# Two stacked transformer blocks on one core: the second layer's norm re-ordered, the last feature weights loaded from ScalarE's queue, the output product's rows ordered by mixer, and weight units dealt by step

## What is computed

```python
hl = xl * (1.0 + scale_l) + shift_l
yl, yc = even_mixer(...)            # layer 0: pooling and a recurrent scan
yl, _ = odd_mixer(...)              # layer 1: attention with a gate
xl = layer_norm(DEEPNORM_ALPHA * xl + gate_l * yl, ln_g[l], ln_b[l])
```

```python
q, k, v, g, lr, u_f, u_h, u_s = jnp.split(rms_norm_2(x, norm_g[l, 0]) @ w_in[l], split_at, axis=-1)
mix = jnp.concatenate([y_a, y_b, y_c, y_d], axis=-1)   # gated linear attention, Fourier, hyena, short convolution
x = x + mix @ w_out[l]
x = x + cross_attention(rms_norm_2(x, norm_g[l, 1]), mem_n, w_xq[l], w_xkv[l], w_xo[l])
x = x + swiglu(rms_norm_2(x, norm_g[l, 2]), w_gate_up[l], w_down[l])
return rms_norm_2(x, final_norm_g)
```

## Time and profile before

| what | value |
|---|---|
| time, median of 3 runs (lowest, highest) | 3949.34 us (3944.61 to 3950.49) |
| the profiled execution's own time | 3950.59 us |
| its span | 3948.7 us |
| TensorE busy with products | 3620.2 us (92%) |
| VectorE, ScalarE, GpSimd busy | 2022.7 (51%), 1541.9 (39%), 272.2 us (7%) |
| TensorE's mean granted clock (1 is full speed) | 0.962 |
| DMA traffic | 548.76 MB, 139 GB/s over the span |

### The profile page before, as it was taken

The page is one execution under the profiler, slowest core; times in us unless marked ns, Lnnn a source line. Parts: engine busy times, 40 slices in busy tenths (PEclk is TensorE's granted clock), DMA queues, the critical chain, the costliest instruction groups (busy, mean ns, idle before and its releaser), DMA issues. The chain is left out here.

```text
span 3948.7 us, 73924 instructions
## 1 busy us (share of the span) xinstructions
PE 3620.2 (92%) x32796; PEld 2974.7 (75%) x32796; DVE 2022.7 (51%) x3453; ACT 1541.9 (39%) x2586; POOL 272.2 (7%) x311
## 2 busy tenths in 40 slices
PE   6789999999898998989989799888999999999998
PEld 3566676767676676767678688846989799999887
DVE  1444454444445447675565546656544455555444
ACT  1333343333333333354454444334543444444343
POOL 0001110111011113012000000100000000000000
PEclk8899999999999999989999899989999999999999
DMA  9523333242333406443224444323554445555554
GB/s 322 179 78 94 105 90 115 69 125 72 117 105 92 129 19 251 141 139 103 89 97 161 144 150 144 124 92 126 178 183 144 159 163 184 185 179 187 187 186 155
DMA packets 349484, 548.76 MB, mean 139 GB/s; under 512 B 11724, under 2 KB 119916, under 8 KB 346988
## 3 DMA queue, kind: packets, MB, share of 16 engines
q1 hardware_dynamic: 346860, 539.83, 42.4%
q10 hardware_dynamic: 2304, 4.20, 0.3%
HBM read 535.86 MB, written 8.13 MB: 138 GB/s over the span
## 5 line engine op out<-in xcount | busy, mean ns | idle before, releaser
L301 PE MATMUL lane<-r,r 128*128 128x256 f32 (+1 forms) x8520 | 1500.4, 325 | 31.8 <-DVE r L259 25.4
L301 PE MATMUL bank<-r,r 128*128 128x512 f32 (+2 forms) x6360 | 1407.0, 360 | 43.1 <-DVE r L259 34.5
L259 DVE TENSOR_TENSOR r<-ring,r 128x1024 fp32r<-128x1024 f32 x773 | 947.9, 1233 | 944.0 <-ACT r L298 942.7
L301 PEld LDWEIGHTS lane<-r,r 128*128 128x128 f32 x8520 | 1259.2, 190 | 205.2 <-DVE r L259 34.4
L301 PEld LDWEIGHTS bank<-r,r 128*128 128x128 f32 x6360 | 1049.5, 194 | 259.9 <-issue 55.5
L298 ACT ACTIVATE r<-ring 128x1024 fp32r<-128x1024 f32 x773 | 810.5, 1055 | 955.4 <-PE lane L301 555.5
L301 PE MATMUL lane<-arena 64*64 64x64 f32 (+5 forms) x13708 | 667.9, 249 | 60.1 <-issue 24.0
L301 PEld LDWEIGHTS lane<-arena 64*64 64x64 f32 (+3 forms) x13708 | 505.0, 139 | 209.2 <-issue 126.3
L298 ACT ACTIVATE arena<-lane 128x256 f32<-128x256 f32 (+3 forms) x578 | 252.7, 457 | 582.9 <-PE lane L301 484.0
L270 DVE COPY arena<-lane 128x256 f32<-128x256 f32 (+3 forms) x366 | 131.7, 362 | 307.5 <-PE lane L301 304.4
L259 DVE TENSOR_TENSOR arena<-arena 128x256 f32<-128x256 f32 (+6 forms) x546 | 253.6, 495 | 27.7 <-ACT arena L298 14.8
(11 more groups left out here) (93 smaller groups left out, 1328.6 us busy)
## 6 DMA issues: line engine op xcount, KB each, us to landing
ring<-in_mod_w SPq DMA_DIRECT2D x96, 1024.0 KB, 5.4
ring<-in_w_gate_up SPq DMA_DIRECT2D x88, 1024.0 KB, 5.1
ring<-in_ev_w_in SPq DMA_DIRECT2D x44, 1024.0 KB, 8.6
ring<-in_w_down SPq DMA_DIRECT2D x44, 1024.0 KB, 5.2
ring<-in_od_w_in SPq DMA_DIRECT2D x40, 1024.0 KB, 5.1
ring<-in_w_in SPq DMA_DIRECT2D x40, 1024.0 KB, 5.1
ring<-in_w_xkv SPq DMA_DIRECT2D x32, 1024.0 KB, 5.2
ring<-in_ev_w_out SPq DMA_DIRECT2D x28, 1024.0 KB, 5.0
```

The source lines that it names most:

```text
L259: return Nothing() if self.e is None else self.e.tensor_tensor(o, a, b, op)
L301: return Nothing() if self.e is None else self.e.matmul(o, l, r, start=start, stop=stop)
```

## The change

Parts, in the order of the list:

1. `Group.rot` becomes a list of starts (`order`). For the first block's product it is the same order as before; for `w_out_2` it is blocks 0, 4, 12, 8 in place of 12, 0, 4, 8.
2. The norm: the first tile is aggregated and scaled behind its last residual, its root is finished within the second tile's last residual. The gains run tile by tile. ScalarE squares quarters of 512 columns, each behind its gain. The two sums and both roots of the RMS norm are taken together. The fence `block2` becomes a mark, on which SP and GpSimd wait in `load_mix`.
3. The convolutions of `uh_in` become steps of their own (`uh_conv`): chores for the first two groups, four steps behind the product for the third. `local_mixers` yields its share of units with each step. The splits of the mixed rows wait for the hyena's input product (mark `first_norm_read`) and, from block 12 on, for `sc_out`; four of them stand ahead of the last convolutions. The filter's steps move one unit later, and two units instead of three stand behind `hy_norm`.
4. Two units of the key product instead of one stand ahead of the norm.
5. `load_fg` moves behind the down product's first column group and is issued by ScalarE. `x_gain` multiplies by the gain, ahead of the root, for the first three column groups, as chores.
6. At the end, `last_sum` takes the sums and roots of both tiles, then VectorE scales 1536 columns of the first tile, ScalarE 1536 of the second, VectorE the last 512 of both; SP stores 1536 and 512 columns.

```diff
-    def __init__(self, act_, kt, tiles, w, c0, n, kind, args, done, is_feats, rot):
+    def __init__(self, act_, kt, tiles, w, c0, n, kind, args, done, is_feats, order):
...
+        self.order = order or list(range(0, kt, 4))
+    def row(self, k):
+        return self.order[k // 4] + k % 4
...
-    step("fence", "block2")
+    step("mark", "block2")
...
-    drain(normed("hF0", "xk", 0, turn_all, ("norm1",)))
+    drain(normed("hF0", "xk", 0, turn_all, ("norm1",), summed=True))
...
+    def uh_done(n):
+        def f():
+            if n < 2:
+                for i in range(4):
+                    chores.append(later(step, "uh_conv", i, n))
+        return f
...
             for g2 in range(2):
                 step("fn_channels", tl, g2, bank(aux))
-                yield
+                yield 1
         for tl in range(2):
             step("fn_tokens", tl, bank(aux))
-            yield
+            yield 1.2
...
         for f in range(4):
             step("sc_conv", f)
-            yield
+            yield 0.9
+        yield 2.4
         b = bank(aux)
         step("sc_sum", b)
-        yield
+        yield 0.5
         step("sc_root", b)
-        yield
+        yield 2.6
         step("sc_out", b)
 
-    weave(local_mixers(), to_hyena, 1.5)
+    weave(local_mixers(), to_hyena)
...
-                        (lambda: step("x3_done")) if n == 3 else None, 12) for n in range(4)], Turn([0, 1, 2, 3]), (2, 12))
+                        (lambda: step("x3_done")) if n == 3 else None, [0, 4, 12, 8]) for n in range(4)], Turn([0, 1, 2, 3]), (2, 12))
...
     drain(to_hyena)
+    step("mark", "first_norm_read")
+    splits(4)
+    for f in range(4):
+        step("uh_conv", f, 2)
     step("local_done")
     step("mark", "hyena")
...
     def hyena():
-        splits(4)
+        splits(2)
         yield 1
         splits(2)
         yield 1
-        step("hy_one", bank(hy_turn))
-        splits(2)
-        yield 1
-        step("hy_two", bank(hy_turn))
         splits(2)
         yield 1
         splits(2)
+        step("hy_one", bank(hy_turn))
+        yield 1
+        step("hy_two", bank(hy_turn))
+        yield 1
...
         for tl in range(2):
             step("hy_norm", tl)
-        yield 3
+        yield 2
...
     next(kv)
+    next(kv)
     weave(normed("hF16", "xk", 16, aux, ("x3",)), kv, 1)
...
-    groups[-1].done = lambda: step("load_fg")
...
+            if n == 0:
+                step("load_fg")
+            if n < 3:
+                chores.append(later(step, "x_gain", n))
...
+    finish_chores()
+    for tl in range(2):
+        step("last_sum", tl)
     for tl in range(2):
         step("finish", tl)
```

In VectorE's program:

```diff
+        st = M.st2[:, 32 * tl:32 * tl + 32]
+        residual(M.xk[:, tl, n * 512:n * 512 + 512], b, M.gb1, st, n,
+                 (lambda: norm_root("norm1", 0, M.st2[:, 0:32])) if (tl, n) == (1, 3) else None)
+        if n == 3:
+            norm_root_in("norm1", tl, st)
...
-        norm_roots("norm1", [M.st2[:, 32 * tl:32 * tl + 32] for tl in range(2)])
-        for q in range(4):
-            for tl in range(2):
-                norm_gain("norm1", q, tl, M.xk[:, tl, :], M.lng1, M.lnb1)
+        for i, (tl, q) in enumerate((tl, q) for tl in range(2) for q in range(4)):
+            if i == 1:
+                norm_root("norm1", 1, M.st2[:, 32:64])
+            norm_gain("norm1", q, tl, M.xk[:, tl, :], M.lng1, M.lnb1)
...
+    def x_gain(n):
+        c_ = slice(512 * n, 512 * n + 512)
+        v.wait_ge(*at("fg"))
+        for tl in range(2):
+            v.wait_ge(*at("sq", "x5", n, tl))
+            v.tt(M.xk[:, tl, c_], M.xk[:, tl, c_], M.fg[:, c_], MUL).then_inc(*v.n(("x_gain", n, tl)))
```

In ScalarE's program:

```diff
-            split(name, k, ("fence", "hyena", "pe"), ("sc_out",))
+            split(name, k, ("fence", "first_norm_read", "pe"), *([("sc_out",)] if k >= 12 else []))
...
+        for q in range(4):
+            x(0, q)
+        x(1, 0)
+        for q in range(1, 4):
+            x(1, q)
+            norm1_square(0, q - 1)
+        norm1_square(0, 3)
+        for q in range(4):
+            norm1_square(1, q)
...
+    def load_fg():
+        a.wait_ge(*at("gate_up_read"))
+        a.dma(M.fg, row(M.I["final_norm_g_2"])).then_inc(*a.n(("fg",), sem="ld_fg", by=16))
...
+    def finish(tl):
+        if tl == 1:
+            a.wait_ge(*at("x_gain", 2, 1))
+            a.wait_ge(*at("fin_pow", tl))
+            a.act(M.xk[:, tl, 0:1536], M.xk[:, tl, 0:1536], ACT.Copy, scale=M.st2[:, 41 + 2 * tl:42 + 2 * tl]) \
+                .then_inc(*a.n(("result", tl, 0)))
```

More of the change, by code:

```diff
@@ L1026, in out_groups @@
     def out_groups(tiles, ns):
-        return [rows("mix", KT, tiles, "ev_w_out", n * 512, 512, "add_first", (n,), None, 8) for n in ns]
+        return [rows("mix", KT, tiles, "ev_w_out", n * 512, 512, "add_first", (n,), None, [8, 12, 0, 4]) for n in ns]
     out_lat = stream(out_groups([2, 3], [1]) + out_groups([2, 3, 0, 1], [0]) + out_groups([2, 3], [2, 3]), out_turn, (2, 8))
@@ L1239, in gla @@
             step("to_mix", "gla", 0, j, bank(aux))
-    to_hyena = stream([feats("hF0", KT, "w_in_2", W2_H + 512 * n, "uh_in", (n,)) for n in range(3)], st_turn)
+    def uh_done(n):
[4 more added lines that the diff above has]
+        return f
+    to_hyena = stream([feats("hF0", KT, "w_in_2", W2_H + 512 * n, "uh_in", (n,), uh_done(n)) for n in range(3)], st_turn)
     def beside_gla():
@@ L1267, in local_mixers, with splits @@
             step("sc_conv", f)
-            yield
+            yield 0.9
+        yield 2.4
         b = bank(aux)
         step("sc_sum", b)
-        yield
+        yield 0.5
         step("sc_root", b)
-        yield
+        yield 2.6
         step("sc_out", b)
-    weave(local_mixers(), to_hyena, 1.5)
+    weave(local_mixers(), to_hyena)
     fill = stream([rows("mF", KT, [0, 1], "w_out_2", n * 512, 512, "add_x", ("x3", n, None),
-                        (lambda: step("x3_done")) if n == 3 else None, 12) for n in range(4)], Turn([0, 1, 2, 3]), (2, 12))
+                        (lambda: step("x3_done")) if n == 3 else None, [0, 4, 12, 8]) for n in range(4)], Turn([0, 1, 2, 3]), (2, 12))
     hy_turn = Turn([4, 5, 6, 7])
+    early = [0, 1, 2, 3, 4, 5, 6, 7, 12, 13, 14, 15]
+    def splits(n):
+        for _ in range(n):
+            step("split", "mF", early.pop(0))
     drain(to_hyena)
+    step("mark", "first_norm_read")
+    splits(4)
+    for f in range(4):
+        step("uh_conv", f, 2)
     step("local_done")
@@ L1284, in order_of_work @@
     step("hy_load")
-    early = [12, 13, 14, 15, 0, 1, 2, 3, 4, 5, 6, 7]
-    def splits(n):
-        for _ in range(n):
-            step("split", "mF", early.pop(0))
     def hyena():
-        splits(4)
+        splits(2)
         yield 1
@@ L1382, in order_of_work, with down_done, f @@
                    feats("hF32", KT, "w_gate_up_2", DFF + 512 * n, "ff_up", (n,))]
-    groups[-1].done = lambda: step("load_fg")
-    groups += [rows("ff", FT, [0, 1], "w_down_2", n * 512, 512, "add_x", ("x5", n, 1)) for n in range(4)]
+    def down_done(n):
+        def f():
+            if n == 0:
+                step("load_fg")
+            if n < 3:
+                chores.append(later(step, "x_gain", n))
+        return f
+    groups += [rows("ff", FT, [0, 1], "w_down_2", n * 512, 512, "add_x", ("x5", n, 1), down_done(n)) for n in range(4)]
     feed_forward = stream(groups, Turn(list(range(8))))
@@ L1502, in load_mem @@
         load("mem", M.memx, I["mem_2"][0].rearrange("(t p) n -> p t n", p=P))
-    def load_fg():
-        sp.wait_ge(*sp.table.at("gate_up_read"))
-        load("fg", M.fg, row(I["final_norm_g_2"]))
     def finish(tl):
@@ L2412, in gate_diag, with residual @@
                 .then_inc(*v.n(("gate_diag", l, side_, q)))
-    def residual(xs, b, gate, stats, n):
+    def residual(xs, b, gate, stats, n, between=None):
         v.tt(M.bank[b[0]], M.bank[b[0]], gate[:, n * 512:n * 512 + 512], MUL).then_inc(*v.n())
@@ L2417, in residual @@
         v.stt(xs, xs, ALPHA, M.bank[b[0]], MUL, ADD).then_inc(*v.n(("free", *b)))
+        if between:
+            between()
         own()
@@ L2579, in rms @@
         if summed:
-            v.wait_ge(*at("at_rms", dst, tl, "act"))
-            v.wait_ge(*at("at_rms", dst, tl))
+            if after[0] == "norm1":
+                sums = range(2) if tl == 0 else ()
+                for i in sums:
+                    for q in range(4):
+                        v.wait_ge(*at("norm1_sq", i, q))
+            else:
+                sums = (tl,)
+                v.wait_ge(*at("at_rms", dst, tl, "act"))
+                v.wait_ge(*at("at_rms", dst, tl))
             own()
-            v.add_up(c, M.st2[:, 44 + 4 * tl:48 + 4 * tl]).then_inc(*v.n())
+            for i in sums:
+                v.add_up(M.st2[:, 4 * i:4 * i + 1], M.st2[:, 44 + 4 * i:48 + 4 * i]).then_inc(*v.n())
             own()
@@ L2586, in rms @@
             v.wait_ge(*at("rms_sq", dst, tl))
-        root(r, c, 1.0 / D, RMS_EPS, "rms_in", dst, tl)
```

(7 more changed lines are left out.)

74 lines of the change are left out of this document (44 added, 30 removed).

## The result

The changed kernel takes **3922.46 us** in the median of 4 runs (3918.92 to 3929.13), against 3949.2 for the kernel before in runs beside it: a ratio of 0.9931, with an interval of 0.9914 to 0.9947. That is faster by 0.69%. Forecast were 3929.1 us and a range of 3919.5 to 3940.5. Its profiled execution took 3925.52 us, with a span of 3923.7, 25.0 less than the span before.

What follows compares the result with a forecast made beforehand. TensorE, busy 92% of the span, was taken as the bound, so only its gaps could be won. Terms -5.0 - 9.4 - 4.0 + 0 - 6.5 + 5.8 - 1.1 = -20.2 us gave 3929.1 us from the median 3949.34; range 3919.5 to 3940.5.

Steps and rivals of the forecast that it cites:

- Part 1, -5.0 us: Second layer's norm: earlier first-tile root and quarter squares let transposes start at 2246.5, not 2251.49; bounds -3.5 and -6 us.
- Part 2, the taps, -9.4 us: Mixers' end and hyena's filter: VectorE's queue lets the taps' products start at 2580.9, not 2590.35; ends -4 and -12 us.
- Part 2, two units instead of three, -4.0 us: Behind the hyena's norm: transposes follow at once instead of waiting for a third unit; bounds 0 and -4.1 us.
- Part 3, 0: Cross attention's norm: a second key unit ahead only moves the 3.33 us gap; ends 0 and -3.3 us.
- Part 4, -6.5 us: Change-over to the down product: load leaves SP's queue, so the 4.83 us gap and 1.7 us of clock go.
- rival to part 4: Change-over to the down product stays late: only issue time, 0.34 us, is gained; 3935.3 us; chance 0.06.
- Part 5, +5.8 us: Down product's first column group: x_gain waits for the weights, 4.1 us idle plus 1.7 of clock; ends 0 and +8.1.
- Part 6, -1.1 us: Kernel's end: operands ready by 3942, but stores bound it, the last landing at 3947.1; ends 0 and -4 us.
- The likeliest case: Whole kernel: all terms sum to -20.2 us, giving 3929.1 us; own range 3924 to 3935, chance 0.53.
- none of the rivals: Features in time 0.17; hyena's start unmoved 0.17; late change-over 0.06; VectorE bounds mixers 0.04; little change 0.03.
- signs of being wrong: Forecast wrong if new gap missing or over 8 us, taps under 10 us earlier, or clock below 1 within mixers.
- the rival for which that sign stood: Mixers: VectorE becomes the bound and TensorE's clock falls, up to 49 us more; 3958 us; chance 0.04.

Runs made afterwards that it cites:

- Runs 5: The norm's change alone, on the kernel before: norm gap 19.90 us, not 25.17; from TensorE's restart to the turned low-rank rows 21.38 us, not 24.52.
- run 6: The mixers' change alone, on the kernel before: turned low-rank rows to taps 303.68 us (before 314.34), taps to transposes behind the hyena's norm 97.31 (before 102.39).
- Run 8: run 1 with 136 identity transposes on TensorE ahead of the norm's first transposes: restart to turned low-rank rows 21.24 us, 0.1 less.
- run 7: Kernel before with two sets of 40 identity transposes on TensorE in the gaps at the mixers' end: mixers' sum to taps 33.15 us, not 37.47.
- run 1: Changed kernel with its first two gains one output group later: first down product to last product 247.52 us, not 254.73; whole 3921.66 us.
- run 3: run 1 with the final norm's weights loaded from SyncE's queue behind the last up product, as before: first down product to last product 253.38 us.
- run 4: Changed kernel with the old finish, without x_gain, load still on ScalarE's queue: last product to span's end 11.81 us against 10.00; whole 3925.42 us.
- run 10: run 1 with one unit of keys ahead of the cross attention's norm, not two: gap 3.53 us.
- run 11: Changed kernel with the final norm's weights loaded five units into the down product's first column group and one more key unit behind the second tile's norm step: 3924.57 us.
- run 9: run 2 with TensorE's mark for the load set behind the last up product: first down product to last product 247.53 us.
- run 12: Changed kernel unaltered, measured again beside run 11: 3928.59 us, 0.9946 of before.
- run 2: run 1 with the final norm's weights loaded from SyncE's queue, still behind the down product's first column group: first down product to last product 254.10 us.

## Why the prediction held, step by step

**Part 1, -5.0 us: -5.3, and 3.1 more that it had no term for.** The steps of the norm held one by one. The clock behind the stop was left out, although the prediction priced the same effect at 1.7 us at three other places. Runs 5 and 6 put the 3.1 us in this part. The windows show them as clock: the upper level begins 1.5 us sooner behind the restart and lasts 2 us longer from there, some 3.4 us more of it in all. Run 8 shows that a busier TensorE in the stop doesn't add to it. Why the level is held longer behind the shorter stop stays open.

**Part 2, the taps, -9.4 us: -10.8.** The input product's end was forecast 2.0 us earlier (+1.2 - 1.5 - 1.7) and came 1.5 earlier: its last product was over at 2559.30 before and at 2550.22 after, 283.3 and 281.8 us behind the turned low-rank rows. From there to the first sine 15.3 us were forecast and 13.9 measured, to the taps 23.6 and 21.8. The step said that TensorE's units fit beneath and don't set the end. In the kernel before they did set it in part: run 7 gets 3.3 of these us by keeping the clock up alone. The size was nearly right, the account of where the old time had gone was not whole.

**Part 2, two units instead of three, -4.0 us: -4.0** behind the cut in run 6. The step that failed is "from the taps to the hyena's norm the chain stays as it is": with four splits of the rows fewer between the filter's steps the gap of 1.85 us is gone, which is worth 1.1 us. In the changed kernel's first profile another 1.2 came on top, from the clock alone. It falls at the taps in every profile, and how long it stays down changes between runs of the same code: ahead of the cut the kernels with part 2 had 0.91 in 37.2 to 37.6 us, 0.83 in 39.7 (runs 1, 3 and 4) and 0.79 in 39.76 (run 6), and their C was 94.5 to 97.3 us. These 1.2 us are chance as far as is known.

**Part 3, 0: 0.** The gap is 3.32 us with two units ahead of the norm and 3.53 with one (run 10): a unit ahead of the norm only moves it. One behind the second tile's norm step breaks it up, into 0.83 and 1.79 (run 11), and that is bounded by the weights' splits.

**Part 4, -6.5 us: -5.9** by run 3 against run 1. 0.81 us of the 4.83 stayed, and the forecast had taken off all of it. Issued by SyncE behind a wait that is already met, the same load costs 0.01 us more than from ScalarE (run 9). That agrees with the Trainium skill, DMA: Bandwidth & Descriptors, section Issuing engines are not separate DMA queues. As a rival to part 4 its rule would have missed by 5.6 us, since what the change removed was a wait.

**Part 5, +5.8 us: +7.2** by run 1, +6.2 in run 12. The chain is the forecast's: load behind the column group, wait, late split of the third unit, TensorE dry, clock. Two of its terms were mis-sized. The load left 1.2 us behind the group's last product (3722.85 against 3721.63), not 2.0: ScalarE issued it while its second square was still running. And it took 7.1 us to land, not 5.3, near the 7.7 that stood as the upper end. The gap is 5.05 for 4.1, the clock 2.2 for 1.7.

**Part 6, -1.1 us: -1.8** by run 4, bounded by the stores as forecast, at 400 GB/s.

The likeliest case came and none of the rivals. The sum, -20.2, is 4.8 short of the -25.0 between the two spans: 3.1 in stretch A, 2.3 in C, 1.4 in B, 0.7 at the end and 0.4 in the rest came on top, 2.2 in the down product and 0.9 ahead of the norm went the other way. So part of the closeness is luck: terms that were left out (3.1 of clock, 1.1 of splits) and terms that were mis-sized partly cancel. The median of 3922.46 us lies below the likeliest case's own range of 3924 to 3935, within the wide one; the second median of the same kernel, 3928.59 (run 12), lies in both. Of the signs of being wrong, the new gap is 5.05 us, between its two bounds, and the taps start 18.4 us earlier, over the 10. The third, a clock below 1 within the mixers, came in the letter: 0.66 in the 5 us from 2466 on, at the end of the linear attention. But the kernel before has the same 0.66 there, from 2482 on, and through the short mixers, from 2471 to 2572, it is 1.00 in the changed kernel's first profile: the rival for which that sign stood did not come. (It can fall there for a moment: to 0.72 over 6 us from 2525 and again from 2556 in run 2, whose stretch B is the long one, and to 0.66 over 5 us from 2558 in run 12.) The claim that 0.2% can be told from no change was too good for one part: medians of 5 or 6 runs did not show 7 us that the trace shows.

## What to carry to other kernels

A wait in the queue that feeds the weights costs by its place, not by the transfer behind it; before a step is moved, look up what its mark on the other engines will then mean (run 2), and give a mark that guards a buffer a step of its own (run 9). A gain or scaling taken off the tail needs its operand long before: VectorE is in order, and 7 us at one wait became 7 us of TensorE. Where a program's early part scatters by 10 us, compare profiles by stretches between named events of TensorE, not by totals, and begin the windows of both profiles at the same event. Before a shorter stretch is put down to the clock, compare the granted clock over it: in run 6 it was the same, and a gap was gone.

## What the runs showed of the hardware that was not expected

TensorE's granted clock was 0.50 while the engine was busy without a break, on products of 32 columns with 128x128 weights (windows from 2259.09 after and from 2263.49 before), so a full row of busy digits doesn't mean the upper level of 2.4 GHz. It was 1.00 over 15 us of nothing but transposes of the identity, was still 1.00 through the gap of 5.06 us behind them and 0.57 in the 4 us after that (run 8): there the loss fell on the work behind the gap. And the same code, from the taps to the first turned rows, took 37.2 us at a clock of 0.91 in run 2 and 39.7 at 0.83 in run 1.
